# One product matmul for the high and low weights side by side, and the stick-breaking half of the branch product moved into the sparse attention

## What is computed

```python
def stick_breaking_block(start, q, k, v):
    z = jnp.einsum('bqhd,bkhd->bhqk', qb, k) * (D_HEAD ** -0.5)
    ...
    a = jnp.where(visible, jnp.exp(jax.nn.log_sigmoid(z) + excl), 0.0)
    return jnp.einsum('bhqk,bkhd->bqhd', a, v)          # o_sb, 8 heads of 64

def dsa_block(start, q, k, v, q_idx, k_idx, w_idx, k_top):
    ...
    p = jax.nn.softmax(logits, axis=-1)                  # over the selected keys
    return jnp.einsum('bhqk,bqkhd->bqhd', p, vg)         # o_ds, 8 heads of 64

def hybrid_mixer(h, ...):
    ...
    merged = gate_sb * (o_sb @ w_branch_sb) + gate_ds * (o_ds @ w_branch_dsa)
    return merged @ w_out
```

## Time and profile before

| | us |
|---|---|
| median of 3 runs | 1741.37 (1740.12 to 1743.99) |
| the profiled execution | 1746.8 |
| its span, first to last instruction | 1745.0 |
| first half of the attention | about 193 to 722 |
| second half | about 722 to 904 |
| its tail | 904 to 918.3 |
| branch stage | 918.3 to 1008.4 |
| product with `w_out`, norms, MLP | 1008.4 to 1745.0 |

### The profile page before, as it was taken

The page is one execution under the profiler, slowest core; times in us unless marked ns, Lnnn a source line. Parts: engine busy times, 40 slices in busy tenths (PEclk is TensorE's granted clock), DMA queues, the critical chain, the costliest instruction groups (busy, mean ns, idle before and its releaser), DMA issues. The chain is left out here.

```text
span 1745.0 us, 23454 instructions
## 1 busy us (share of the span) xinstructions
PE 1638.4 (94%) x8360; PEld 1384.4 (79%) x8360; DVE 1245.4 (71%) x1966; ACT 851.5 (49%) x1650; POOL 539.7 (31%) x332
## 2 busy tenths in 40 slices
PE   4999899999999999889889999989999999999997
PEld 4889888799877777777777878768888878888885
DVE  5287798888988989687873435785454548777878
ACT  5266555555445545576751133555555543333334
POOL 1111254555434435321102450475545510000000
PEclk6999999999999999998989999999999999999999
DMA  4564434344233233355304443243444365443434
GB/s 172 155 194 124 128 120 134 108 137 114 89 106 107 92 106 107 91 134 135 86 1 163 139 169 121 72 158 133 145 149 174 136 229 217 157 159 131 169 138 103
DMA packets 101372, 231.23 MB, mean 133 GB/s; under 512 B 11192, under 2 KB 25848, under 8 KB 101256
## 3 DMA queue, kind: packets, MB, share of 16 engines
q1 hardware_dynamic: 100680, 227.64, 40.7%
q0 software_dynamic: 576, 2.10, 0.7%
HBM read 155.83 MB, written 73.86 MB: 132 GB/s over the span
## 5 line engine op out<-in xcount | busy, mean ns | idle before, releaser
L710 PE MATMUL bk<-x_hi,w_hi 128*128 128x512 f32 (+2 forms) x832 | 308.7, 371 | 1.2 <-PEq L353 1.2
L710 PE MATMUL bk<-x_lo,w_hi 128*128 128x512 f32 (+2 forms) x832 | 299.3, 360 | 0.0
L710 PE MATMUL bk<-x_hi,w_lo 128*128 128x512 f32 (+2 forms) x832 | 298.5, 359 | 0.0
L666 POOL TENSOR_TENSOR pt_lo<-a_buf,pt_hi 128x512 fp32r<-128x512 f32 (+3 forms) x104 | 138.4, 1347 | 193.0 <-ACT pt_hi L930 192.8
L334 POOL TENSOR_TENSOR w_lo<-w_raw,w_hi 128x1024 fp32r<-128x1024 f32 x53 | 130.4, 2460 | 190.9 <-ACT w_hi L330 190.7
L1087 DVE TENSOR_SCALAR_CACHE_REDUCE counted<-sc,small 128x272 uint8<-128x272 f32 (+6 forms) x217 | 182.5, 891 | 0.9
L1674 PE MATMUL bank<-v_hi,f_hi 128*128 128x512 f32 x448 | 174.3, 389 | 0.0
L1674 PE MATMUL bank<-v_hi,f_lo 128*128 128x512 f32 x448 | 174.3, 389 | 0.0
L1674 PE MATMUL bank<-v_lo,f_hi 128*128 128x512 f32 x448 | 174.3, 389 | 0.0
L710 PEld LDWEIGHTS bk<-x_hi,w_lo 128*128 128x128 f32 x832 | 158.5, 191 | 17.6
L710 PEld LDWEIGHTS bk<-x_hi,w_hi 128*128 128x128 f32 x832 | 159.1, 191 | 16.1 <-issue 1.3
(11 more groups left out here) (228 smaller groups left out, 3861.0 us busy)
## 6 DMA issues: line engine op xcount, KB each, us to landing
w_raw<-w_units SPq DMA_DIRECT2D x57, 512.0 KB, 3.7
f_raw<-f_d SPq DMA_DIRECT2D x28, 1024.0 KB, 5.0
u_raw<-w_units SPq DMA_DIRECT2D x32, 512.0 KB, 4.8
f_d<-f_s SPq DMA_DIRECT2D x64, 256.0 KB, 2.2
b<-w_units SPq DMA_DIRECT2D x16, 1024.0 KB, 8.3
f_d<-c SPq DMA_DIRECT2D x48, 256.0 KB, 2.1
k_hi<-k_d SPq DMA_DIRECT2D x32, 260.0 KB, 5.6
k_lo<-k_d SPq DMA_DIRECT2D x32, 260.0 KB, 6.1
```

Of the source, the lines that this page charges most:

```text
L666: pool.tensor_tensor(pt_of(pt_lo, j, tiles), raw, pt_of(pt_hi, j, tiles).bitcast(F32), ALU.subtract).then_inc(sb_lo, 1)
L710: mm = pe.matmul(pj[b][:, 0:c1 - c0], w[:, s, kt, :], a[:, kt, c0:c1], start=kt == 0 and k == 0, stop=kt == KT - 1 and k == 2)
```

## The change

One: `pt_hi` and `pt_lo` of a pair become the two halves of one buffer `pt`, and a slot is one matmul that streams both past the values, into twice the columns (a whole PSUM bank of 512). The output of a product is now four parts, high and low weights by high and low values, instead of two.

Two: these four parts are added elsewhere. ACT copies all of a bank into `o_st`, which is now one buffer, and SP stores it (256 KB); this is done for the first 56 products, the sparse heads' too, and only the last pair of heads is added up in SBUF (`add_rest`, three additions). ACT waits for the store of product `k - 1` before it copies product `k`, and it copies ahead of `round_weights` instead of at the step's end. Seven pairs are loaded back, at steps 66, 70, 75, 80, 85, 101 and 117, each as eight loads: parts 0 and 1 at the step itself, part 2 a step later and part 3 two steps later. All parts but the first go through one buffer `o_raw[1]`, so SP waits for POOL's addition before it loads the next, and POOL adds three times. ACT rounds the sum of a stick-breaking pair four steps after the first load. The sparse pairs are scaled at 90, 106, 122 and 129.

Three: the stick-breaking half of the branch product (16 parts of 128 x 512, 12 matmuls each) is dealt evenly over steps 86 to 125. Bank 0, which transpositions used too, holds it. SP loads the gates, DVE multiplies, SP stores the gated part to `m1_d`, a step after the part's end and behind the head load where there is one. The branch stage multiplies only the sparse half, 24 matmuls for each `k`, and DVE adds the loaded `m1_d` where POOL added before.

```diff
-RELOAD = [NJ // 2 + 6 + 10 * p_ for p_ in range(4)]
-PAIR_AT = [NJ // 2 + 16 * (p_ + 1) + 4 for p_ in range(3)] + [NJ + 1]
+RELOAD = [(NJ // 2 + step_, p_) for step_, p_ in ((2, 0), (6, 1), (11, 2), (16, 3), (21, 4), (37, 5), (53, 6))]
+PAIR_AT = [NJ // 2 + 16 * (p_ + 1) + 10 for p_ in range(3)] + [NJ + 1]
+K_LAST = 4 * H + 24
...
-    ring = (4, 5, 6) if j < NJ // 2 + 2 else (4, 5, 6, 0)
     TPN[key] = len(TP_BANK)
-    TP_BANK.append(min(ring, key=...
+    TP_BANK.append(min((4, 5, 6), key=...
...
+PARTS = 2 * KT
+B_STEPS = [(j_, part_) for j_ in range(NJ // 2 + 22, NJ - 2) for part_ in range(2)]
+for n_ in range(4 * PARTS):
+    j_, part_ = B_STEPS[n_ * len(B_STEPS) // (4 * PARTS)]
+    B_FILL[j_][part_].append(divmod(n_, 4))
...
+                def load_piece(n, x):
+                    p = RELOAD[n][1]
+                    s, half = divmod(x, 2)
+                    if x == 0:
+                        sp.wait_ge(o_spilled, 16 * 8 * (p + 1))
+                        if n == 0:
+                            in_dram(U_BRANCH - 1)
+                        if 1 <= p < 4:
+                            sp.wait_ge(or_lo, p)
+                    elif n or x > 1:
+                        sp.wait_ge(or_sum, 3 * n + x - 1)
+                    dst = o_raw[1] if x else o_raw[0] if p < 4 else o_pair[p - 4]
+                    for g in range(2):
+                        sp.dma_start(dst[DH * g:DH * g + DH], o_d[2 * p + g, s, DH * half:DH * half + DH, :]).then_inc(or_in, 16)
...
-                        if j == RELOAD[p] + 1:
-                            pool.wait_ge(or_in, 64 * (p + 1))
-                            pool.tensor_tensor(o_raw[0][:], o_raw[0][:], o_raw[1][:], ALU.add).then_inc(or_sum, 1)
+                        if step < j <= step + 3:
+                            x, whole = j - step, o_raw[0] if p < 4 else o_pair[p - 4]
+                            pool.wait_ge(or_in, 128 * n + 32 * (x + 1))
+                            if x > 1:
+                                pool.wait_ge(or_sum, 3 * n + x - 1)
+                            pool.tensor_tensor(whole[:], whole[:], o_raw[1][:], ALU.add).then_inc(or_sum, 1)
...
+                def branch_part(m, h):
+                    u, k, c = part_at(m)
+                    if h == 0:
+                        if m == 0:
+                            pe.wait_ge(or_lo, 4)
+                            bank_read(NC_ALL - 2 + NC_ALL % 2)
+                        else:
+                            pe.wait_ge(part_gated, m)
+                        pe.wait_ge(lo_done, u + 1)
+                    for n, (w, a) in enumerate(((w_hi, o_hi), (w_hi, o_lo), (w_lo, o_hi))):
+                        mm = pe.matmul(bk[0][:], w[:, u % 2, 4 * (k % 2) + h, :], a[:, h, c * HALF:(c + 1) * HALF], ...
...
-                        for w in (hi, lo):
-                            mm = pe.matmul(dst, v_hl[0:r, g % 2, slot, :], w[0:r, cols], start=slot == 0 and w is hi,
-                                           stop=slot == o + 1 and w is lo)
+                        mm = pe.matmul(dst, v_hl[0:r, g % 2, slot, :], whole[0:r, :, cols], start=slot == 0, stop=slot == o + 1)
...
-                        if k >= 2:
-                            act.wait_ge(o_spilled[k % 2], 16 * (k // 2))
-                        act.copy(o_st[:, k % 2], o_part(k)).then_inc(o_free, 1)
+                        if k:
+                            act.wait_ge(o_spilled, 16 * k)
+                        act.copy(o_st[:], o_part(k)).then_inc(o_free, 1)
...
-                def reload(p):
-                    act.wait_ge(or_sum, p + 1)
+                def reload(n, p):
+                    act.wait_ge(or_sum, 3 * n + 3)
                     act.copy(o_hi[:, p, :], o_raw[0][:]).then_inc(or_hi, 1)
...
                     if p < 3:
-                        dve.wait_ge(o_free, 4 * H + 8 * (p + 1))
+                        dve.wait_ge(or_sum, 3 * [q for _, q in RELOAD].index(4 + p) + 3)
...
+                def gate_part(m):
+                    dve.wait_ge(gate_sb_in[m % 2], 16 * (m // 2 + 1))
+                    if m >= 2:
+                        dve.wait_ge(m1_out[m % 2], 16 * (m // 2))
+                    dve.wait_ge(part_mm, m + 1)
+                    dve.tensor_tensor(m1_st[:, m % 2], bk[0][:], gate_sb[:, m % 2], ALU.mult).then_inc(part_gated, 1)
```

More of the change, by code:

```diff
@@ L989, in _ @@
                         evacuate(n)
-                    for p in range(4):
-                        if j == RELOAD[p] + 3:
-                            reload(p)
+                    for m in B_ENDS[j][1]:
+                        next_unit(m)
+                    for n, (step, p) in enumerate(RELOAD):
+                        if j == step + 4 and p < 4:
+                            reload(n, p)
                     if j > NJ // 2 and j % 16 == 0:
                         spread((j - NJ // 2) // 16 - 1)
-                    for k in OUT_AT[j]:
-                        output(k)
                     for p in range(3):
```

200 lines of the change are left out of this document (128 added, 72 removed).

## The result

The changed kernel takes **1826.7 us** (median of 4 runs, 1823.1 to 1830.1) against 1742.2 us for the kernel before beside it (4 runs, 1740.1 to 1744.0). The ratio is 1.0485, 95% interval 1.0461 to 1.0509: slower by 4.9%. The forecast was 1794 with a range from 1760 to 1832, so the sign and the range hold and the middle is 33 us short. The profiled run has a span of 1824.3 us, 79.3 us more than the earlier trace rows.

What follows compares the result with a forecast made beforehand. It took PE to bound the branch stage and nearly the first attention half, with PE waiting for others in the second. Terms +60 + 23 + 18 + 5 - 8 - 45 = +53 us on the 1741.4 median gave 1794 us, range 1760 to 1832.

Steps and rivals of the forecast that it cites:

- The reload chain: Steps 64 to 86: one-buffer load and sum rounds cost 27.4 us a stick-breaking pair, step 86 near 849, +60 us.
- Sums of the sparse pairs: After step 86: DVE waits for reloaded sums at steps 90, 106 and 122, +23 us (9 to 32).
- The branch matmuls: Steps 86 to 125: 45.0 us of added PE work only partly hides in idle time, +18 us (11 to 30).
- The store of one buffer: Four heads from step 89 on: ACT's copy waits some 2 us for a store behind a head load, +5 us (0 to 16).
- One matmul for two: First half's 32 products: merged matmuls save 0.16 to 0.25 us each, -8 us (-2 to -12).
- The branch stage: Branch stage, PE alone: 192 matmuls fewer at 0.234 us, -45 us (-43 to -46).
- The clock: TensorE in the second half: stalls lower it for a few matmuls, fill removes drops after step 86, 0 (-3 to +8).
- B: Rival for the second half: the reload stays hidden, faster, about 1706 us; chance 0.08.
- E: Rival: enough of the stall runs in the shadow of other waits, 1738 to 1760 us; chance 0.05.
- D: Rival for the reload: shorter rounds, two loads in 4.1 us and four in 5.3, 1771 us; chance 0.10.
- C: Rival in SP's queue: held-back stores also make ACT's copies wait, 1822 us, up to 1840; chance 0.15.
- A: The forecast itself: reload sets the pace from step 70 to 86 and at three later steps, 1778 to 1815; chance 0.62.

Runs made afterwards that it cites:

- the dealt half alone: Kernel before with only the stick-breaking half of the branch product dealt over steps 86 to 125, without the merged matmul, stores and reload of old size: 1749.2 us.
- the ring alone: Kernel before with one edit, three transposition banks instead of four in the second half: 1755.1 us, ratio 1.0084.
- the split kernel: Changed kernel with each slot of a product again two matmuls, for high and low weights, into the column halves of one bank: 1834.6 us, ratio 1.0531.

## Why the prediction was right, and where not

The sign and the cause ahead of step 86 are right. That the total lies in the range is in part luck: behind step 86, terms that were nothing and costs that had been put at little or nothing nearly cancel, and the parts have to be judged one by one.

- **The reload chain (+60, measured +63.1): right, mechanism and size.** Additions are 6.9 us apart, the first two low parts 27.6 us apart, the fourth low part is done at 847.8 where 849 was said. Three buffers took 27 us off, as the chain's own sum says (4 x 7.0 = 28). The closeness to 849 has luck in it: the first low part was done at 758.4 and not at 762.2, 3.8 us early, and the third pair's late start gave 3.7 us back; and with its own -8 us for the first half the sum would have had step 86 at 841. ACT's waits for the sum, announced at 10 to 17 us each, were 7.4, 13.5 and 3.8: a part of the standing still sat in ACT's waits for stores instead.
- **Sums of the sparse pairs (+23, range 9 to 32): failed.** DVE waited 0.7 us. The term priced SP's rounds of 24 to 25.5 us against steps of 16.5 to 20 us; the steps took so much longer for other reasons (67.0 us from step 90 to 106) that the sums were there just in time. Waits that run beside each other can't be added: when one makes the steps longer, the other is hidden. With two slots for the stores the hidden one came out, 8.3 us of DVE's waiting.
- **The branch matmuls (+18, range 11 to 30): inside the range on the dealt half alone, and nothing in this kernel.** With stores and reload of the old size they cost 21.6 us. In the changed kernel, taking out 176 of them moved nothing.
- **The store of one buffer (+5, range 0 to 16): mis-sized.** A second slot gave back 16.8 us in steps 86 to 127. The forecast counted four heads at some 2 us, which makes 8 and not the 5 that it put down; the profile shows five waits of up to 5.8 us, 20.5 in all, four for a store behind a head load and one (3.9 us) behind a pair's loads and a unit of weights.
- **What was costed at nothing.** DVE's gating was put at nothing against 20 additions saved; the gate loads and stores and the units' rounding stand in no term; the ring of three banks was a reason for 18 us within 11 to 30 and nothing ahead of step 86. Without the 176 matmuls, the dealt half alone still took 14.2 us more in steps 86 to 127, 3.7 of them at most the 16 matmuls left (16 x 0.234), and 6.7 more in steps 64 to 86. In the kernel before, the ring alone made 2.4 and 3.8 us of this. How the rest divides was not measured.
- **The account of the +58.7 us, by runs.** Second slot -16.8, more buffers on top -8.1, matmuls on top of that -10.7, and 23.1 that none of them removes. On the dealt half alone 14.2 us stay without the matmuls; that the same 14.2 are in the 23.1 is likely and not shown. The order matters: taken out first, the matmuls would stand here with 0. The forecast's 46 for these steps is thus near the 58.7 by errors of opposite sign: 23 for sums that cost nothing, against 16.8 for stores put at 5 and a side work put at nothing.
- **One matmul for two (-8; 2.2 by PE's timeline, step 64 2.6 us earlier): mis-sized,** by the 16-row slot, put at 0.23 to 0.32 us and measured at 0.42. In the second half the split kernel was 6.4 us longer, by one profile of each; the forecast had 4 us of this inside the term of the branch matmuls.
- **The branch stage (-45): right,** -44.3. The clock (0, up to +8) can't be separated: the changed kernel's mean is 0.948 against 0.972, and the run without the matmuls has a mean of 0.940 at the same time.
- **Rivals.** B and E fell. D fell: two loads took 4.6 us at POOL. The Trainium skill's "DMA: Bandwidth & Descriptors", Anatomy of one DMA, would have two in 3.2 us, by a fit that the page gives for DMAs issued by GpSimd; here SP issues them, 64 rows each, and the trace shows 4.5 to 4.8 us from buffer free to data there. C's time, 1822 to 1840, is the measured one, and its mechanism is shown: two slots bring the kernel to 1809.1, into A's 1778 to 1815. Its sum takes three upper ends as separate mishaps; the trace shows one cause, SP's list worked off in order, in which stores and loads wait for one another, and a store's lateness then holds both ACT and SP. But the price by C's mechanism was paid behind step 86 (16.8 us) and hardly ahead of it (1.4 us), and C added it on top of A's other terms, two of which were nothing.

## What to carry to other kernels

A chain of load, sum, load in one buffer can be summed from a few rows: a pair came to 27.6 us where 27.4 was forecast. What fills the time beside it can't be added term by term. Where an engine is busy for 85% of a stretch, ask first whether others wait in it at the same time: taking its work out for one run (the same waits, one matmul of each part left) says whether it is the bound. And count the room that a filler takes as well as its work: a PSUM bank, a place in the queue, the other engines' side work; here moving half of the product out of a stage of 90 us saved 44 there, and what it needed on the way cost at least as much in every version that does the whole work.

## What the runs showed of the hardware

- **Cutting PE's work lowered its granted clock in steps 86 to 127, each time.** 0.91 to 0.77 in the changed kernel, where the time stayed as it was; 0.99 to 0.86 in the one with more buffers and two slots (12.7 us less in the whole), 0.98 to 0.91 on the dealt half alone (22.7 us less). The Trainium skill's "TensorE: Matmul & The Clock Gate", Part 1, says that the throttled state is the default and activity releases it; the three pairs agree. Busy time of PE is therefore no measure of its work where the clocks differ: 41 us of matmuls less (176 at 0.234) made it fall by 22.6 us in the changed kernel.
- **Loads of 64 rows and 256 KB, one buffer:** two are there 4.5 to 4.8 us after POOL has freed it, in 7 of the 8 later rounds of the four pairs (8.3 us with a head load in between).
- **A matmul of 16 rows and 512 columns** takes 0.42 us to the next start, as much as two of 256 columns, where one of 128 rows and 512 columns takes 0.24 (30 products of the first half, before and after).
- **Stores behind loads in SP's queue** land at up to 7.8 us after their issue, for 256 KB, with a median of 2.7 over all 56.
